# Input norm folded through the projection's split products, and decode attention with the cache as the moving operand in column tiles

## What is computed

```python
def rmsnorm(x, g):
    y = x * lax.rsqrt(jnp.mean(x * x, axis=-1, keepdims=True) + RMS_EPS)
    return y * g

xn = rmsnorm(x, g_mix)
u = xn @ w_in                     # 58 tiles of 128 columns feed RWKV, mLSTM and pooling; the gate columns come later

q = (xn @ wq).reshape(B, L, XA_HEADS, XA_HEAD_DIM)          # 4 heads of 128
s = jnp.einsum('blhd,bmhd->bhlm', q, mem_k) * (XA_HEAD_DIM ** -0.5)
p = jax.nn.softmax(s, axis=-1)
o = jnp.einsum('bhlm,bmhd->blhd', p, mem_v).reshape(B, L, XA_WIDTH) @ wo
```

## Time and profile before

| | |
|---|---|
| median of three runs | 2316.16 us (2315.3 to 2322.4) |
| profiled execution | 2316.09 us, of which 2314.3 us lie between first and last instruction |
| projection, first block's start to POOL's last add | 0 to 417 us |
| mLSTM with pooling | 418 to 586 us |
| cross-attention up to its output tiles | 1661.8 to 1738.4 us |
| experts, from their norm on | 1767 to 2314 us |
| PE busy | 2044.3 us (88%) |

### The profile page before, as it was taken

The page is one execution under the profiler, slowest core; times in us unless marked ns, Lnnn a source line. Parts: engine busy times, 40 slices in busy tenths (PEclk is TensorE's granted clock), DMA queues, the critical chain, the costliest instruction groups (busy, mean ns, idle before and its releaser), DMA issues. The chain is left out here.

```text
span 2314.3 us, 32838 instructions
## 1 busy us (share of the span) xinstructions
PE 2044.3 (88%) x13030; PEld 1648.2 (71%) x13030; DVE 855.7 (37%) x1419; ACT 575.8 (25%) x900; POOL 289.2 (12%) x290
## 2 busy tenths in 40 slices
PE   6999999699799999999999799999988877777775
PEld 5999999566577677777777699999987633333332
DVE  4333333323534434335335444456313411111113
ACT  4333333101221211212212333334212211111112
POOL 3000000442212112022021000272000000000000
PEclk8999999555899999999999899999958888898888
DMA  6443431112231130221212244544604499999994
GB/s 256 155 180 146 181 145 73 58 75 77 92 120 53 66 120 36 83 80 76 83 73 83 78 164 164 223 178 187 237 1 177 170 428 428 429 428 428 428 428 184
DMA packets 36213, 409.11 MB, mean 177 GB/s; under 512 B 5428, under 2 KB 7224, under 8 KB 10936
## 3 DMA queue, kind: packets, MB, share of 16 engines
q1 hardware_dynamic: 36152, 408.25, 43.8%
HBM read 397.06 MB, written 11.18 MB: 176 GB/s over the span
## 5 line engine op out<-in xcount | busy, mean ns | idle before, releaser
L971 PE MATMUL ps<-xn,ring 128*128 128x288 f32 x1024 | 273.5, 417 | 21.1 <-ACTq L1157 10.8
L361 PE MATMUL ps<-x_high,w_high 128*128 128x288 f32 x928 | 252.1, 297 | 16.7 <-ACT w_high L260 11.6
L971 PEld LDWEIGHTS ps<-xn,ring 128*128 128x128 f32 x1024 | 191.1, 193 | 89.5 <-issue 15.0
L362 PE MATMUL ps<-x_rest,w_high 128*128 128x288 f32 x928 | 251.6, 299 | 0.0
L318 DVE TENSOR_TENSOR w_rest<-ring,w_high 128x2048 fp32r<-128x2048 f32 x58 | 134.1, 2313 | 231.3 <-ACT w_high L260 231.3
L2187 PE MATMUL ps<-ring,xg 128*32 128x512 f32 x1024 | 149.7, 737 | 71.1 <-DMA ring<-in_w_egu 71.1
L361 PEld LDWEIGHTS ps<-x_high,w_high 128*128 128x128 f32 x928 | 176.5, 190 | 17.9 <-ACT w_high L260 12.1
L362 PEld LDWEIGHTS ps<-x_rest,w_high 128*128 128x128 f32 x928 | 176.6, 190 | 0.0
L260 ACT ACTIVATE w_high<-ring 128x2048 fp32r<-128x2048 f32 x58 | 111.0, 1913 | 217.7 <-PE ps L362 217.7
L2187 PEld LDWEIGHTS ps<-ring,xg 128*32 128x32 f32 x1024 | 38.7, 131 | 158.8 <-issue 118.3
L366 PE MATMUL ps<-x_high,w_rest 128*128 128x288 f32 x928 | 134.1, 297 | 0.0
(11 more groups left out here) (523 smaller groups left out, 3760.4 us busy)
## 6 DMA issues: line engine op xcount, KB each, us to landing
ring<-in_w_egu SPq DMA_DIRECT2D x64, 2048.0 KB, 20.6
ring<-in_w_ed SPq DMA_DIRECT2D x32, 2048.0 KB, 20.5
ring<-in_w_main SPq DMA_DIRECT2D x29, 2048.0 KB, 7.4
ring<-in_w_gate SPq DMA_DIRECT2D x24, 2048.0 KB, 7.6
ring<-in_w_up SPq DMA_DIRECT2D x8, 2048.0 KB, 7.6
ring<-in_w_out SPq DMA_DIRECT2D x8, 2048.0 KB, 7.6
ring<-in_w_up_rw SPq DMA_DIRECT2D x8, 1024.0 KB, 6.8
ring<-in_c_in SPq DMA_DIRECT2D x4, 1024.0 KB, 5.9
```

The costliest lines, as they stand in the source:

```text
L361: mm(ps[:, n, 0:T], high[:, n % 2, k, :], x_h[:, k, :], start=(k == 0), stop=False)
L362: ins = mm(ps[:, n, 0:T], high[:, n % 2, k, :], x_l[:, k, :], start=False, stop=False)
L971: ins = mm(ps[:, 0, 0:T], w[b][:, t, d * P:(d + 1) * P], xn[:, t, :], start=(t == 0), stop=(t == n - 1))
```

## The change

Two parts, both in the diff.

1. The gain is applied as the input is rounded (`x_high` by ACT, `x_rest` by DVE), the products run on the unnormalised input, and the inverse root `rstd` is multiplied in when a bank is evacuated, now by DVE. The squares are summed by POOL while the first tiles run, one matmul after tile 4 sums them over the partitions, and DVE evacuates tiles 0 to 3 together after that, then each tile two behind the one whose rest it makes. The final adds into `xn` go; instead mLSTM loads `xT` a second time, and DVE normalises four blocks of it for each head (new L745).
2. The decode unit moves from ninth to fifth place. Its queries are spread into zeroed blocks of 32 columns (`qs`), its probabilities likewise (`psq`), and the cache becomes the moving operand: 256 keys or 128 value columns at a time, against 32 stationary columns, the four heads in four groups of 32 output partitions, summed over sequences in PSUM. The result comes out with queries as rows; ACT copies it to `seen`, and PE transposes it once.

Smaller: the wait for `again` in the merge stage moves behind `rest_out(1)`, buffers get other places, and POOL zeroes `qs` (merge stage) and `psq` (cross stage).

```diff
@@ projection
-                sp.dma_start(mrg[:, 4 * n:4 * n + 4, :], A["xT"][:, 4 * n:4 * n + 4, :]).then_inc(x_in[n], 16)
-            sp.dma_start(param[:, :], A["param"][:, :]).then_inc(loaded, 16)
+            sp.dma_start(param[:, :], A["param"][:, :]).then_inc(loaded, 16)
+            for n in range(4):
+                sp.dma_start(x[:, 4 * n:4 * n + 4, :], A["xT"][:, 4 * n:4 * n + 4, :]).then_inc(x_in[n], 16)
...
+                nc.scalar.activation(x_h[:, k, :], x[:, k, :], ACT.Copy, scale=par("g_mix", k)).then_inc(x_high, 1)
+            for n in range(SUM_AFTER + 3):
+                split(n, 0)
+            act.wait_ge(variance, 1)
+            nc.scalar.activation(rstd[:, :], rstd[:, :], ACT.Sqrt).then_inc(rooted, 1)
...
+                    ins = stt(out=o, in0=src, scalar=scale, in1=by, op0=ALU.mult, op1=ALU.mult)
...
+                stt(out=x_l[:, k, :], in0=x[:, k, :], scalar=par("g_mix", k), in1=x_h[:, k, :], op0=ALU.mult,
+                    op1=ALU.subtract).then_inc(x_rest, 1)
...
-            nc.vector.tensor_tensor(xn[:, 0:KH, :], x_h[:, 0:KH, :], x_l[:, 0:KH, :], ALU.add)
...
-            nc.gpsimd.tensor_tensor(xn[:, KH:KD, :], x_h[:, KH:KD, :], x_l[:, KH:KD, :], ALU.add)
...
             for n in range(8):
+                if n == 7:
+                    pe.wait_ge(variance, 1)
                 tile(n, 0)
+                if n == SUM_AFTER:
+                    pe.wait_ge(one_set, 1)
+                    pe.wait_ge(squares, 2 * KD - 1)
+                    mm(ps[:, 7, 0:T], one[:, :], rstd[:, :], start=True, stop=True).then_inc(summed, 1)
@@ mLSTM
+                if h == 1:
+                    sp.dma_start(xn[:, :, :], A["xT"][:, :, :]).then_inc(again, 16)
...
                 if h + 1 < MLH:
                     weights(h + 1)
+                if h == 0:
+                    dve.wait_ge(again, 16)
+                for k in range(4 * h, 4 * h + 4):
+                    stt(out=xn[:, k, :], in0=xn[:, k, :], scalar=par("g_mix", k), in1=rstd[:, :], op0=ALU.mult, op1=ALU.mult)
                 dve.wait_ge(a.sem, a.at(f"cp{h}"))
@@ cross-attention
-        order = [(h, c) for h in range(XH) for c in range(2)] + [None]
+        order = [(h, c) for h in range(XH) for c in range(2)]
+        order.insert(4, None)
...
                 if order[j] is None:
-                    pe.wait_ge(a.sem, a.at("sT"))
-                    for m in range(2):
-                        ins = nc.tensor.transpose(ps[:, bank, m * P:(m + 1) * P], sT[:, m, :], ident)
+                    for b in range(NB):
+                        for h in range(XH):
+                            n = h * 256 + b * NSM
+                            ins = mm(ps[h * NSM:(h + 1) * NSM, bank, 0:MEM], qs[:, n:n + NSM], kc[h // 2][:, h % 2, b, :],
+                                     start=(b == 0), stop=(b == NB - 1))
...
-                                ins = mm(o[:, n:n + NL], vc[m][:, b, h, :], pt[:, j % 2, m, n:n + NL], start=(m == 0), stop=(m == 1))
+                                ins = mm(ps[h * NSM:(h + 1) * NSM, 4 + j % 2, 0:P], psq[:, m, h, b * NSM:(b + 1) * NSM], vc[m][:, b, h, :],
+                                         start=(b == m == 0), stop=(b == NB - 1 and m == 1))
...
-                if j < 5:
-                    decode_scores(j)
...
+                if j == 5:
+                    act.wait_ge(q.sem, q.at("o4"))
+                    a.done(fn(seen[:, :], ps[:, 4, 0:P], ACT.Copy), "seen")
```

More of the change, by code:

```diff
@@ L214, in stage_project @@
         x_rest = sem("p_x_rest")
-        v = Steps(ctx, nc, "p_vec", ["var", "rstd"] + [f"xn{k}" for k in range(KD)])
+        variance, inverse = sem("p_var"), sem("p_inverse")
         w_high = sem("p_w_high")
@@ L284, in _ @@
[L284 to L295, removed]
@@ L301, in _ @@
+            act.wait_ge(variance, 1)
+            nc.scalar.activation(rstd[:, :], rstd[:, :], ACT.Sqrt).then_inc(rooted, 1)
+            split(SUM_AFTER + 3, 0)
+            with act.Fori(1, ITER) as i:
+                for n in range(8):
+                    split(n, i)
+            for n in range(2):
+                split(n, ITER)
         @block.vector
         def _(dve):
-            dve.wait_ge(summed, KD)
-            v.done(nc.vector.tensor_scalar(rstd[:, :], ps[:, 7, 0:T], 1.0 / D, RMS_EPS, ALU.mult, ALU.add), "var")
@@ L305, in _ @@
[L305 to L311, removed]
-            for k in range(KD):
-                v.done(nc.vector.scalar_tensor_tensor(out=low(k), in0=mrg[:, k, :], scalar=par("g_mix", k),
-                                                      in1=rstd[:, :], op0=ALU.mult, op1=ALU.mult), f"xn{k}")
+            tt, stt = nc.vector.tensor_tensor, nc.vector.scalar_tensor_tensor
@@ new lines, in evacuate_one @@
+            def evacuate_one(t):
+                if t == 40:
+                    dve.wait_ge(carried, 1)
+                evacuate(t, outputs(t), t % 8, DQK ** -0.5 if 28 <= t < 32 else 1.0)
+            dve.wait_ge(loaded, 16)
+            for k in range(KD):
+                dve.wait_ge(x_high, k + 1)
+                stt(out=x_l[:, k, :], in0=x[:, k, :], scalar=par("g_mix", k), in1=x_h[:, k, :], op0=ALU.mult,
+                    op1=ALU.subtract).then_inc(x_rest, 1)
+            for n in range(SUM_AFTER + 2):
+                rest(n, 0)
@@ new lines, in _ @@
+            dve.wait_ge(summed, 1)
+            nc.vector.tensor_scalar(rstd[:, :], ps[:, 7, 0:T], 1.0 / D, RMS_EPS, ALU.mult, ALU.add).then_inc(variance, 1)
+            dve.wait_ge(rooted, 1)
+            nc.vector.reciprocal(rstd[:, :], rstd[:, :]).then_inc(inverse, 1)
+            dve.wait_ge(inverse, 1)
+            for t in range(SUM_AFTER):
+                evacuate_one(t)
+            for n in range(SUM_AFTER + 2, 8):
+                rest(n, 0)
+                evacuate_one(n - LAG)
+            with dve.Fori(1, 3) as i:
@@ L1475, in stage_merge @@
     places = env["cross"]
-    mkt, mv, qt, wide_h = (places[k] for k in ("mkt", "mv", "qt", "high"))
+    mkt, mv, qt, qs, wide_h = (places[k] for k in ("mkt", "mv", "qt", "qs", "high"))
     kc, vc = places["kc"], places["vc"]
@@ L1865, in _ @@
             sp.wait_ge(caches["kv_out"], 32)
+        @block.gpsimd
+        def _(pool):
+            nc.gpsimd.memset(psq[:, :, :, :], 0.0).then_inc(cleared, 1)
         @block.tensor
@@ L1928, in _ @@
                     values(j - 1)
+                if j == 6:
+                    pe.wait_ge(a.sem, a.at("seen"))
+                    q.done(nc.tensor.transpose(ps[:, 4, P:2 * P], seen[:, :], ident), "seen")
             values(8)
@@ L1956, in results @@
             def results(j):
-                act.wait_ge(q.sem, q.at(f"o{j}"))
+                act.wait_ge(q.sem, q.at("seen" if order[j] is None else f"o{j}"))
                 src, out = attended(j, ot_h)
```

175 lines of the change are left out of this document (94 added, 81 removed).

## The result

The changed kernel took 2262.36 us, the median of four runs (2261.24 to 2267.11), against 2319.28 for the kernel before beside it (2315.3 to 2323.0): a ratio of 0.9759, with a 95% interval from 0.9733 to 0.9784. Measured once more, in a later batch, it was 2263.5, ratio 0.9761 (0.9735 to 0.9787). The first medians lie 56.9 us apart; the forecast was 43.9. The profiled execution of the changed kernel took 2267.11, its span is 2265.3, so the two traces that are compared here lie only 49.0 apart. Both gaps to the forecast, 13 us by medians and 5 by traces, have to be explained.

A forecast was written before the change was run, and what follows sets the result against it. PE was taken to wait on the norm at the projection's start and end, and to spend long on decode products with 4 moving columns. 2316.1 - 25.1 + 5.0 - 23.8 = 2272.2 us; range 2262 to 2287.

The forecast's parts named there:

- Part 1a and 1b: Projection's start and end: tile 1 18.7 us earlier, 0.5 for the matmul over ones, end 6.9 shorter; together 25.1 won.
- rival (c): Projection: POOL's sum of squares comes late, its instructions over 1.51 us each; at 1.9, 2284.4 in all; chance 0.05.
- Rival (d): Projection's start: late weights, so the change does not bring tile 0 forward; no chance of its own stated.
- Part 1c: mLSTM: DVE's added normalising delays state products by 1.3 us in three heads, plus 1.1 for the clock; 5.0 lost.
- the term of 5.0: mLSTM's whole forecast loss: 3.9 us of waits in three heads and 1.1 for the clock; range 3 to 10.
- the 1.1 for the clock: mLSTM's state products: a wait ahead may turn a quick head slow, 0 to 2.3 us for each of two; 1.1 taken.
- Part 2: Cross-attention: decode scores at 6.5 us and values at 9.0, output tiles at 1714.6 instead of 1738.36; 23.8 won, range 15 to 31.
- The sentence that leaned on the experts' row: Decode values in the attention: 70 ns each, 9.0 us, nearer the experts' row (0.204 for 512 columns), which has the same groups.
- steps 1 and 3: Attention, between transpositions t0 and t1, and t2 and t3: forecast from 1664.6 to 1667.3 and from 1676.5 to 1680.0.
- The two steps with weight blocks: Attention, steps to t4 and t6, where an output weight block is also rounded: 7.01 us, and 15.2 with the decode values.
- Rival (a): Attention: every narrow instruction costs the upper 0.125 us; 8.5 us more, 2280.7 in all; chance 0.12.
- rival (b): Attention: the column groups do not run side by side; 62.9 us more, 2335, slower than before; chance 0.04.

The follow-up runs named there:

- the attention alone: The decode attention in column tiles alone, projection and mLSTM as in the kernel before: 2287.86 us, ratio 0.9849 to the kernel before.
- the doubled values: The changed kernel with the 128 decode value products made twice: the doubled group 2.2 to 3.0 us longer than the single one, the attention 77.4 us.
- the head-major order: The changed kernel with decode scores and values issued head after head, neighbours in the same output group: the attention takes 92.4 us, some 15 more.

## Why the prediction was right, and too cautious

**Part 1a and 1b, right.** Forecast 25.1, measured 25.2, with errors that cancel. The weights' first rounding began at 15.04, not 14.2, and ACT loaded a table for 1.28 us ahead of its first instruction, which the sum had left out. The rests cost 0.884 instead of the 0.985 taken; PE waited 1.48 of the 2.0 allowed. Tile 1 came at 27.09 for the 26.3 forecast, 17.9 won of 18.7. The matmul over ones cost 0.27 for 0.5. The end, from PE's last product to mLSTM's first, gave 7.73 - 0.77 = 7.0 for 6.9, and the tiles between another 0.6. POOL was done at 40.2, since its instructions took 0.7 to 0.9 beside DVE's short rests and 2.6 only beside weight rests: they took 1.1 on average, and rival (c), which needed 1.51 for each, was never near. Rival (d) fell with 17.00.

**Part 1c, the waits right, the term for the clock wrong in its sign.** The waits ahead of the state products stand in three heads, 1.36, 1.13 and 0.92 us for the 1.3 forecast, and none in the fourth. But the term of 5.0 came out as 1.1 between the two traces, and as about nothing over all of them (172 to 178 after, 172 to 177 before). The step that failed is the 1.1 for the clock: it took the quick 4.92 of the earlier trace rows (the third head had 5.26) as the rule and a fall as the risk. In two more traces of that code, of which the one of the attention alone is shown here, all four products took 7.19; the profile had shown a lucky execution, by 5 us.

```profile
466.66 7.19 PE L582 MATMUL ps<-ring 32*128 32x512 f32 x8
500.69 7.19 PE L582 MATMUL ps<-ring 32*128 32x512 f32 x8
```

In the changed code more products ran raised, not fewer (21 of 32 against 2 of 12), and that paid for the waits; why is open.

**Part 2, the mechanism right, the size wrong.** Forecast 23.8 up to the output tiles, measured 29.6 in the first trace and 29.6 to 31.8 in five others of the same attention. Two steps of the working were too dear. First the price of the decode values, 0.070 us taken between 0.051 and 0.125: it is 0.047 at the low clock. The sentence that leaned on the experts' row was right and should have gone the whole way. Second, the clock: the working carried the 0.50 of the earlier trace rows over the whole attention. The kernel before had that clock only from about 1668 on, most of it under the decode products that the change replaces, and had 1.00 ahead of that (rows above). In the attention alone the scores ran at the full clock (3.66 for 6.5) and the values raised it towards their end (6.35 for 9.0), together 5.5; steps 1 and 3 were shorter by 1.7. The two steps with weight blocks stand open as forecast, PE idle for 5.0 at 1665.13 and 4.9 at 1680.44. Rival (a) fell with the doubled values, rival (b) with the 3.66; the head-major order shows what (b) would have cost at the clock it was granted, some 15 us and not 63.

**The sum.** The profile of before stood 3 us under the median of its runs (2316.09 for 2319.28), the profile after 5 above (2267.11 for 2262.36), which is 8 of the 13 us between the forecast and the medians; of the trace's own 5.1, the attention gave 5.8 and mLSTM 3.9 more than forecast, RWKV's draw 1.9, and the merge stage took 6.3, of which 5.3 lie in the output tiles with the late POOL. The range from 2262 to 2287 holds the time at its very end, which is partly luck: five of the ten runs of the changed kernel lie under 2262. What the working itself had too dear is the clock, in the attention and in mLSTM.

## What to carry to other kernels

A narrow product was cheap here with the small operand as the stationary one and neighbours in the order in different output groups: what was paid are the moving columns, divided by about the number of groups. When an attention or another chain is shortened, the work that hid under the old long stretch comes to stand open; here two weight blocks cost 16 to 18 us, some 7 of them idle time and the rest with the clock, until they were put under the new, shorter groups. A clock read from the stretch that a change takes away is no price for what comes in its place, and one profile is one draw of every duration that hangs on the clock: two or three traces of the kernel before would have shown the 5 us in mLSTM.

## What the runs showed of the hardware

The order alone makes a factor of 3.1 (0.180 to 0.057 us) in the price of products in different output groups. POOL and DVE slow one another unequally: POOL's squaring of 288 columns takes 0.67 alone, 0.76 beside DVE's short rests and 2.60 beside a weight rest; DVE's short rest goes from 0.434 to 0.884 with POOL at work, its weight rest from 2.29 to about 2.8. And the kernel before spread over 2308.64 to 2324.89 in 13 runs; the traces show spreads of 5 us in mLSTM, with the clock, of 5 in RWKV, only in part with the clock (of the heads in the trace before one took 91.5 us at 0.96 and one 90.8 at 1.00, others 89.2), and single late waits such as POOL's; which of them made a given untraced run long stays open.
